# Expert capacities of 98, 88, 80 and 72 rows by rank, and four expert chunks in unused working memory

## The reference, cut to what matters

```python
def moe_swiglu(u, router_w, w1, w3, w2):
    logits = (tokens @ router_w).astype(F32)
    top_vals, top_idx = lax.top_k(logits, TOP_K)          # TOP_K = 2
    gates = jax.nn.softmax(top_vals, axis=-1)
    ...
    def run_block(args):
        tok_idx, e = args
        xb = tokens[tok_idx]
        return (jax.nn.silu(xb @ w1[e]) * (xb @ w3[e])) @ w2[e]
    ...                                                   # times the gate, added into each token's row
```

## Time and profile before

| | us |
|---|---|
| median of 3 runs (2025.71 to 2027.35) | 2026.94 |
| the profiled execution | 2017.58 |
| its span, first to last instruction | 2015.8 |
| PE busy, share of the span | 1842.4, 91% |
| PEld busy | 1510.7, 75% |
| DVE busy | 826.7, 41% |
| ACT busy | 393.1, 20% |
| DMA, moved | 480.22 MB, mean 238 GB/s |

### The profile page before, as it was taken

One profiled execution on the slowest core, in us unless ns is written; L12 is line 12 of the kernel. 1 busy time (PEld: TensorE's weight loads), 2 busy tenths in 40 slices (PEclk: granted clock), 3 DMA queues, 4 the chain that ended last, 5 costly groups with the idle time before them and its releaser, 6 DMA issues. The chain is left out here.

```text
span 2015.8 us, 43109 instructions
## 1 busy us (share of the span) xinstructions
PE 1842.4 (91%) x18202; PEld 1510.7 (75%) x18202; DVE 826.7 (41%) x2249; ACT 393.1 (20%) x1107; POOL 2.3 (0%) x6
## 2 busy tenths in 40 slices
PE   6999897999989887999999999899979998899987
PEld 4686666888868765789688998698657876688766
DVE  3756552778958812011110111110113676227661
ACT  2232333000014132000000000000012233122331
POOL 0000000000000000000000000000000000000000
PEclk7999998999989887999999999999999999899988
DMA  9622332899973123999999898999993412234100
GB/s 392 238 106 87 123 140 90 312 358 361 378 280 126 42 84 133 420 419 357 373 420 392 315 388 324 421 418 353 363 419 139 167 64 84 84 126 167 43 1 22
DMA packets 67910, 480.22 MB, mean 238 GB/s; under 512 B 7424, under 2 KB 9728, under 8 KB 9856
## 3 DMA queue, kind: packets, MB, share of 16 engines
q1 hardware_dynamic: 67712, 477.39, 60.4%
HBM read 476.31 MB, written 1.05 MB: 237 GB/s over the span
## 5 line engine op out<-in xcount | busy, mean ns | idle before, releaser
L484 PE MATMUL PS<-sb_U,sb_ring 128*128 128x256 f32 (+1 forms) x1456 | 372.6, 413 | 16.3 <-PEq L216 9.9
L484 PEld LDWEIGHTS PS<-sb_U,sb_ring 128*128 128x128 f32 x1456 | 280.7, 196 | 95.6 <-issue 59.4
L1676 PE MATMUL PS<-sb_arena,sb_ring 128*64 128x98 f32 x5632 | 246.3, 247 | 14.3 <-issue 12.2
L1676 PEld LDWEIGHTS PS<-sb_arena,sb_ring 128*64 128x64 f32 x5632 | 240.2, 136 | 21.1 <-issue 18.0
L1704 PE MATMUL PS<-sb_ring,sb_arena 128*64 128x256 f32 x1408 | 161.8, 383 | 5.1 <-issue 4.5
L755 PE MATMUL PS<-sb_U,sb_ring 128*128 128x256 f32 x704 | 155.5, 383 | 4.7 <-PEq L216 4.7
L484 PE MATMUL PS<-sb_arena 128*64 128x128 f32 (+9 forms) x884 | 150.1, 345 | 7.2 <-DVE sb_arena L717 4.4
L755 PEld LDWEIGHTS PS<-sb_U,sb_ring 128*128 128x128 f32 x704 | 134.4, 192 | 25.7 <-issue 7.4
L1704 PEld LDWEIGHTS PS<-sb_ring,sb_arena 128*64 128x64 f32 x1408 | 100.0, 137 | 54.5 <-issue 7.5
L484 PEld LDWEIGHTS PS<-sb_arena 64*128 64x128 f32 (+4 forms) x884 | 106.5, 173 | 45.2 <-issue 24.9
L340 DVE SCALAR_TENSOR_TENSOR sb_arena<-sb_ring,sb_cs,sb_arena 128x256 f32<-128x256 f32 x280 | 135.8, 485 | 10.0
(11 more groups left out here) (343 smaller groups left out, 1615.9 us busy)
## 6 DMA issues: line engine op xcount, KB each, us to landing
sb_ring<-stream SPq DMA_DIRECT2D x450, 1024.0 KB, 7.9
sb_consts<-consts SPq DMA_DIRECT2D x1, 1768.5 KB, 26.6
sb_U<-ctxT SPq DMA_DIRECT2D x1, 1024.0 KB, 6.6
sb_XT<-xT SPq DMA_DIRECT2D x1, 1024.0 KB, 8.4
out<-sb_XT SPq DMA_DIRECT2D x8, 128.0 KB, 2.0
sb_small<-small SPq DMA_DIRECT2D x1, 292.0 KB, 2.9
sb_consts<-consts SPq DMA_DIRECT2D x1, 129.0 KB, 2.8
sb_all_small<-layer_small SPq DMA_DIRECT2D x1, 110.0 KB, 26.8
```

The source lines that it names most:

```text
L484: ins = pe.transpose(o, l, r) if t.turn else pe.matmul(o, l, r, start=s, stop=e)
L1676: ins = pe.matmul(PS[c:c + 64, m % 4, h * T:h * T + n], w[:, h, kt, c:c + 64], src[:, kt, 0:n], start=(kt == 0), stop=(kt == KT - 1))
```

## The change

Three things.

**Capacities.** Ranks 0 to 3 get 98, 88, 80 and 72 rows instead of 98 each. In the order of the places that is 64, 98, 64, 88, 80, 64, 72, 64. The test before the experts counts, for each capacity, how many of the seven counts are above it, and compares with how many ranks have more.

**Four homes.** Chunks 141 to 144, the ones that pw2 used to load into freed slots, get places of their own in the arena (columns 6144, 10752, 13104 and 15968, 2048 each), with a landing semaphore each. They are issued in pw2 with no wait for a slot. Later chunks take the ring's slots as if these four were not in the stream, so pw2 now issues up to chunk 148, and 13 chunks are ready for the experts.

**Two moves.** Column 6144 is now a home, so the turned rows (`UTM`) go to `UC`, the half of `U2` that held the context and is no longer used, in the layout that a rearranged view gives. `GB`, which only `over` uses, goes to column 18016.

```diff
-RANK_CAPS = (98, 98, 98, 98, 64, 64, 64)
+RANK_CAPS = (98, 88, 80, 72, 64, 64, 64)
+STEPS = sorted(set(RANK_CAPS), reverse=True)
+LARGER = [sum(n > step for n in RANK_CAPS) for step in STEPS]
+HOMES = (6144, 10752, 13104, 15968)
+    t["caps"] = np.broadcast_to(np.array(STEPS + LARGER)[None, :], (P, 2 * len(STEPS)))
...
+    def home(self, g):
+        return g - self.home_first if self.home_first <= g < self.home_first + len(self.homes) else None
+    def turn(self, g):
+        return g if g < self.home_first else g - len(self.homes)
     def chunk(self, g):
-        return self.ring[:, (g % RING) * CH:(g % RING + 1) * CH]
+        if self.home(g) is not None:
+            return self.homes[self.home(g)]
+        slot = self.turn(g) % RING
+        return self.ring[:, slot * CH:(slot + 1) * CH]
...
+    def before(self, g):
+        if self.home(g) is not None or self.turn(g) < RING:
+            return None
+        t = self.turn(g) - RING
+        return t if t < self.home_first else t + len(self.homes)
+    def may_issue(self, g, first, end):
+        if g >= self.total:
+            return False
+        if self.home(g) is not None:
+            return first + RING >= self.home_first
+        return self.before(g) is None or self.before(g) < end
     def load(self, sp, first, n, freed):
-        last = min(first + n + RING, self.total)
-        for g in range(self.issued, last):
-            old = g - RING
-            if old >= first and old - first < n:
+        while self.may_issue(self.issued, first, first + n):
+            g, old = self.issued, self.before(self.issued)
+            if old is not None and old >= first:
                 sp.wait_ge(*freed[old - first])
-            sp.dma_start(self.chunk(g), self.dram[self.base + g]).then_inc(self.landed[g % RING], 16)
-        self.issued = max(self.issued, last)
+            sp.dma_start(self.chunk(g), self.dram[self.base + g]).then_inc(self.landing(g), 16)
+            self.issued += 1
...
+        ws = Stream(nc, ring, a["stream"], landed, [area(at, CH) for at in HOMES], home_landed, PRE_CH - OUT_CH + RING)
...
-        UTM = area(6144, 2048).rearrange("p (t n) -> p t n", t=2)
+        UTM = UC.rearrange("p k (t c) -> p t k c", t=2)
...
-                  ("dve", lambda e: e.tensor_scalar(PAIR[:, 0, :], COUNT[:, 1:8], float(HALF), None, ALU.is_gt)),
-                  ("dve!", lambda e: e.reduce_max(MOST, COUNT, AX)),
-                  ("dve", lambda e: e.reduce_sum(KEY[:, 0:1], PAIR[:, 0, :], AX)),
-                  ("dve", lambda e: e.tensor_scalar(KEY[:, 0:1], KEY[:, 0:1], NR - sum(FEW[1:]) + 0.5, None, ALU.is_gt)),
-                  ("dve", lambda e: e.scalar_tensor_tensor(out=KEY[:, 0:1], in0=COUNT[:, 0:1], scalar=float(HALF), in1=KEY[:, 0:1],
-                                                           op0=ALU.is_gt, op1=ALU.max)),
+                  ("dve", lambda e: e.tensor_tensor(PAIR[:, 0:NS, :], COUNT[:, 1:8].unsqueeze(1).broadcast_to([P, NS, NR]),
+                                                    const("caps")[:, 0:NS].unsqueeze(2).broadcast_to([P, NS, NR]), ALU.is_gt)),
+                  ("dve", lambda e: e.reduce_sum(KEY[:, 0:NS], PAIR[:, 0:NS, :], AX)),
+                  ("dve", lambda e: e.tensor_tensor(KEY[:, 0:NS], KEY[:, 0:NS], const("caps")[:, NS:2 * NS], ALU.is_gt)),
+                  ("dve", lambda e: e.reduce_max(MOST, KEY[:, 0:NS], AX)),
```

More of the change, by code:

```diff
@@ L135 @@
            ("cos64", T), ("sin64", T), ("cos32", T), ("sin32", T), ("ncum", TT * T), ("cmask", 3 * P),
-           ("fmask", T), ("bmask", T), ("cmpmask", TT * 16), ("iota", CAP), ("sel16", 16), ("one_of", 63)]
+           ("fmask", T), ("bmask", T), ("cmpmask", TT * 16), ("iota", CAP), ("sel16", 16), ("one_of", 63), ("caps", 2 * len(STEPS))]
 CONST_AT, CONST_N = offsets(CONST_W)
@@ L163, with __init__ @@
 class Stream:
-    def __init__(self, nc, ring, dram, sems):
+    def __init__(self, nc, ring, dram, sems, homes, home_sems, home_first):
         self.nc, self.ring, self.dram, self.landed = nc, ring, dram, sems
+        self.homes, self.home_landed, self.home_first = homes, home_sems, home_first
         self.used = self.issued = 0
@@ L175, in begin, with landing @@
         self.total, self.base = total, base
+    def home(self, g):
+        return g - self.home_first if self.home_first <= g < self.home_first + len(self.homes) else None
+    def turn(self, g):
+        return g if g < self.home_first else g - len(self.homes)
     def chunk(self, g):
-        return self.ring[:, (g % RING) * CH:(g % RING + 1) * CH]
-    def wait(self, eng, g):
-        eng.wait_ge(self.landed[g % RING], 16 * (g // RING + 1))
+        if self.home(g) is not None:
+            return self.homes[self.home(g)]
+        slot = self.turn(g) % RING
+        return self.ring[:, slot * CH:(slot + 1) * CH]
+    def landing(self, g):
+        return self.landed[self.turn(g) % RING] if self.home(g) is None else self.home_landed[self.home(g)]
+    def wait(self, eng, g):
+        eng.wait_ge(self.landing(g), 16 if self.home(g) is not None else 16 * (self.turn(g) // RING + 1))
+    def before(self, g):
[9 more added lines that the diff above has]
+        return self.before(g) is None or self.before(g) < end
     def load(self, sp, first, n, freed):
-        last = min(first + n + RING, self.total)
-        for g in range(self.issued, last):
-            old = g - RING
-            if old >= first and old - first < n:
+        while self.may_issue(self.issued, first, first + n):
+            g, old = self.issued, self.before(self.issued)
+            if old is not None and old >= first:
                 sp.wait_ge(*freed[old - first])
-            sp.dma_start(self.chunk(g), self.dram[self.base + g]).then_inc(self.landed[g % RING], 16)
-        self.issued = max(self.issued, last)
+            sp.dma_start(self.chunk(g), self.dram[self.base + g]).then_inc(self.landing(g), 16)
+            self.issued += 1
         self.used = first + n
     def clear(self):
-        clear_together(self.nc, self.landed)
+        clear_together(self.nc, self.landed + self.home_landed)
 class Stage:
@@ L311, in build @@
         landed = [ctx.enter_context(nc.semaphore(f"landed{i}")) for i in range(RING)]
-        ws = Stream(nc, ring, a["stream"], landed)
+        home_landed = [ctx.enter_context(nc.semaphore(f"home_landed{i}")) for i in range(len(HOMES))]
+        ws = Stream(nc, ring, a["stream"], landed, [area(at, CH) for at in HOMES], home_landed, PRE_CH - OUT_CH + RING)
         late = ctx.enter_context(nc.semaphore("late_inputs"))
@@ L1521, in build @@
         GD = area(10496, 2 * P).rearrange("p (t c) -> p t c", t=2)
-        GB = area(10752, T)
+        GB = area(18016, T)
         YG = area(13104, KT * T).rearrange("p (k t) -> p k t", k=KT)
@@ L1576, in build @@
         rk = area(15152, 560)
-        NR = NE - 1
+        NR, NS = NE - 1, len(STEPS)
         COUNT, KEY, RANK, AT = (rk[:, 8 * i_:8 * i_ + 8] for i_ in range(4))
@@ L1593, in build @@
                   ("dve!", lambda e: e.tensor_copy(COUNT, PS[:, 2, 0:8])),
-                  ("dve", lambda e: e.tensor_scalar(PAIR[:, 0, :], COUNT[:, 1:8], float(HALF), None, ALU.is_gt)),
-                  ("dve!", lambda e: e.reduce_max(MOST, COUNT, AX)),
-                  ("dve", lambda e: e.reduce_sum(KEY[:, 0:1], PAIR[:, 0, :], AX)),
-                  ("dve", lambda e: e.tensor_scalar(KEY[:, 0:1], KEY[:, 0:1], NR - sum(FEW[1:]) + 0.5, None, ALU.is_gt)),
-                  ("dve", lambda e: e.scalar_tensor_tensor(out=KEY[:, 0:1], in0=COUNT[:, 0:1], scalar=float(HALF), in1=KEY[:, 0:1],
-                                                           op0=ALU.is_gt, op1=ALU.max)),
-                  ("dve", lambda e: e.scalar_tensor_tensor(out=full_flag[:, 0:1], in0=MOST, scalar=float(CAP), in1=KEY[:, 0:1],
+                  ("dve", lambda e: e.tensor_tensor(PAIR[:, 0:NS, :], COUNT[:, 1:8].unsqueeze(1).broadcast_to([P, NS, NR]),
[3 more added lines that the diff above has]
+                  ("dve", lambda e: e.reduce_max(MOST, KEY[:, 0:NS], AX)),
+                  ("dve", lambda e: e.scalar_tensor_tensor(out=full_flag[:, 0:1], in0=COUNT[:, 0:1], scalar=float(PLACES[0][1]), in1=MOST,
                                                            op0=ALU.is_gt, op1=ALU.max))]
@@ L1614, in copy_rows @@
                 act.wait_ge(turned, j + 1)
-                nc.scalar.activation(UTM[:, t, 512 * half:512 * half + 512], PS[:, 4 + j, :], ACT.Copy)
+                nc.scalar.activation(UTM[:, t, 4 * half:4 * half + 4, :], PS[:, 4 + j, :].rearrange("p (k c) -> p k c", k=4), ACT.Copy)
         def clear_sum(pool, turned):
@@ L1639, in _ @@
             def _(sp):
-                for g in range(ws.issued, min(last_ch + RING, ws.total)):
-                    old = g - RING - first
-                    if old >= 0:
+                while ws.may_issue(ws.issued, first, last_ch):
+                    g, old = ws.issued, ws.before(ws.issued)
```

(9 more changed lines are left out.)

## The result

The changed kernel took 2010.02 us (median of 9 runs, 2004.16 to 2017.22), the kernel before 2026.89 (9 runs, 2021.53 to 2030.1): ratio 0.9931, 95% interval 0.9914 to 0.9948, or 14 us less (11 to 17). I had forecast 26, with 2001 as the time and 1984 to 2013 as the range. So it is faster, inside the range, and outside the forecast's own range of 1994 to 2008: half of the expected gain is not there.

What follows compares the result with a forecast made beforehand. TensorE and the DMA stream were taken as nearly level bounds, with instruction fetch third; savings of 3.7 + 11 + 5.5 + 0.3 + 5.5 = 26.0 us gave 2001 us, range 1984 to 2013.

Steps and rivals of the forecast that it cites:

- Homes: Place 0, first of eight expert places: four chunks loaded ahead remove 4.85 us of waits, place 1 0.6; sum 5.5 us.
- The third bound: Hidden tiles of places 3 and 6: TensorE waits for instruction blocks, about 6.15 us each behind a full DMA queue.
- The widths: Time of one matmul in places 3, 4 and 6: 38.5, 35.4 and 32.3 ns at 88, 80 and 72 columns.
- Place 6: Expert place cut to 72 rows: hidden tiles set by instruction blocks save about 0, output part 5.5 us.
- Place 3: Expert place cut to 88 rows: hidden tiles save 1 us, output tiles 2.7, sum 3.7.
- Place 4: Expert place cut to 80 rows: hidden tiles near the DMA's pace save 6 us, outputs 4.9, sum 11.
- Rival 2: Instruction fetch slower once TensorE is faster, also in place 4 and outputs: 15 us saved, 2012; chance 0.12.
- Rival 3: Place 4's queue fills, its blocks go to 6.15 us, outputs gain nothing: slower than before, 2029.5 us; chance 0.06.
- Rival 1: Gap is a price per instruction block, or fetch comes faster when asked earlier: 43 us saved, 1984; chance 0.16.

Runs made afterwards that it cites:

- experiment 2: Changed kernel with each experts-stage load bringing only half its columns, TensorE's program the same: 1945.15 us, ratio 0.9604, stage 631.5 for 703.2.
- experiment 5: Changed kernel with 16 more TensorE instructions, waits already met, in each hidden tile of the wide places: 2040.16 us, ratio 1.0082 to the kernel before.

## Why the prediction was half right

- **Homes: right.** Forecast 5.5 us, measured 5.0 in place 0. One wait of 0.56 us stayed of five, where the earlier trace rows had 4.85 us:

```profile
838.20 4.58 PE L1762 MATMUL PS<-sb_ring,sb_arena 128*64 128x128 f32 x78 [0.56 <-DMA sb_ring<-stream]
```

  SyncE issued the four home loads within 2.05 us at the stage's start, and the four of the freed slots after them, as told:

```profile
695.21 2.05 SPq L224 DMA_DIRECT2D sb_arena<-stream  x4
716.89 23.73 SPq L224 DMA_DIRECT2D sb_ring<-stream  x4
```

  The lead did no more later: place 1 is unchanged, where I had hoped for 0.6.
- **The third bound: right** in places 3 and 6, where blocks take 6.0 to 6.4 us with computing of 5.07 and 4.2 (one block takes 6.9); experiments 2 and 5 show that it is the fetch. The widths too: 5.07, 4.65 and 4.22 us for 127 matmuls less the last one's own 0.24 give 38.3, 35.0 and 31.6 ns, forecast 38.5, 35.4 and 32.3.
- **Place 6: near in the sum.** Forecast 5.5, all of it in the output part; measured 3.9, of which the hidden tiles gave 1.1 (65.5 us for 66.6) and the output part 2.8. Blocks of hidden tiles are 6.0 to 6.3 us apart with gaps of 2 us, and those gaps do a thing I had left out:

```profile
1329.51 5.80 PE L1710 MATMUL PS<-sb_arena,sb_ring 128*64 128x72 f32 x127 [2.04 <-issue]
1335.52 4.22 PE L1710 MATMUL PS<-sb_arena,sb_ring 128*64 128x72 f32 x127 [0.22 <-issue]
1341.76 4.17 PE L1710 MATMUL PS<-sb_arena,sb_ring 128*64 128x72 f32 x127 [2.02 <-issue]
```

  127 matmuls took 5.80 us for 4.22. The same columns as the earlier trace rows over the two blocks show why:

```profile
1323.00:1329.00 6.00, 4.22 (x127) 4.07 (x127) 0.91 (x4) 0.73 (x3) 0.00 (x0) 1.00 1.02 422
1329.50:1335.30 5.80, 5.79 (x127) 5.71 (x127) 0.23 (x1) 0.46 (x2) 0.00 (x0) 0.71 1.01 418
```

  The granted clock was 0.71 in the second stretch (between its two levels, 2.4 and 1.2 GHz), after a row of gaps. It costs little here, since the block behind it had arrived meanwhile and its gap is 0.22 us. In the output part blocks still wait, four times for 1.1 to 2.0 us, 5.7 together.
- **Place 3: over-sized.** Forecast 3.7, measured 0.5. The hidden tiles were to give 1 and gave -0.2 (67.6 us for 67.4). The output part was to give 2.7 and gave 0.7: three waits for blocks, of 0.39, 1.53 and 0.16 us, took 2.1 there.
- **Place 4: the step that failed.** I took 11 us: hidden tiles at the stream's 2.50 us each (6), outputs at full computing pace (4.9). It gave 0.7. The hidden tiles stayed at 2.76 us each (60.8 us in all for 60.9) and the outputs took 37.1 us for 37.6. I had seen that the block would get longer as TensorE got faster and that the two would settle at a balance; the error was to price that balance at the stream's pace. It lies at the fetch's: 5.6 us a block, while the stream's queue is only 94% busy, so the stream is not what is late. In the outputs three waits for blocks of 1.2 to 1.3 us took 3.8. One stretch behind the gap of 2.19 us lost time by the clock as well:

```profile
1179.68:1184.90 5.22, 5.22 (x102) 5.22 (x104) 0.24 (x1) 0.26 (x2) 0.00 (x0) 0.67 0.92 363
```

  I had also tied the block's length to a full queue, and that is too simple. The shares of the stream's queue and the blocks seen are: 99.3% and 6.0 to 6.9 us (place 3), 99.6% and 5.9 to 7.2 (three outstanding), 98.1% and 5.5 to 6.1 (two outstanding, place 4), 94.3% and 5.3 to 6.8 (place 4), and 96.9% and no more than 5.4 (place 4 before). The last shows that the share alone doesn't set it, nor does the time to landing, 11.9, 7.6, 5.4, 6.9 and 5.8 us in the same order. What does stays open.
- **Rivals 2 and 3.** Rival 2 (the fetch is late in place 4 and in the outputs too) has the mechanism that was measured, and I had given it 0.12. Its sum of 15 us is near the measured 14 partly by luck: it has 3.7 for place 3, 4 for place 4 and 2 for place 6, where the profile has 0.5, 0.7 and 3.9, and the stage is 10.5 us shorter. Rival 3 did not come: it wanted hidden tiles of 3.07 us and a mean block over 6.0 in place 4, and they are 2.76 and 5.6. The prediction had named the sign of either: place 4 over 95 us (97.8), first gaps there, and issue to landing over 6 us (6.9).
- **Rival 1** (the gap is a price for a block, not a floor of its length) is ruled out beside a full stream: the gap grew from 0.5 to 1.0 to 2.0 us as the block's computing shrank.
- The rule of the Trainium skill that I had weighed (Runtime: NRT & Kernel Launch, Instruction fetch mechanics: the fetch is hidden behind dispatch) agrees with the earlier trace rows, where blocks that compute for 5.4 us run with no gap. The traces of places 3, 4 and 6 after the change disagree with it, by gaps of up to 2.2 us at the blocks' ends.

## What to carry to other kernels

Before you make matmuls narrower in a fully unrolled program that streams its weights, look for gaps at a fixed count of instructions (here 256): they are a floor in time for each block, and below it fewer columns only lengthen the gap. A place that shows no gaps today may just hide the fetch behind its computing (here 5.4 us a block in place 4), and gets them when it becomes faster, with the DMA engines no busier. Loads ahead into idle memory pay at most the waits that stand before them, here 5 us for 10 us of lead.

## What the runs showed of the hardware

- A block of 256 TensorE instructions (16 KB) that TensorE waited for came 4.9 to 7.2 us after the one before, most of them 6.0 to 6.4, where the DMA engines were at least 95% busy (changed kernel; three outstanding). At 79 to 94% it was 4.7 to 6.3 us (experiment 5; three outstanding). At 70% five in a row came in 4.1 us each or less, and single ones still took 5.7 (experiment 2).
- Loads of 512 KB for 1024, cut by columns, left it at 6.1 us, and three loads outstanding for up to seven did not shorten it.
- A stream of loads into 64 partitions each moved 257 GB/s in a full queue, one into 128 partitions 420 GB/s, both in rows of 8 KB. Rows of 4 KB over 128 partitions reached 400 to 420 GB/s in the stretches where the queue was full.
- Behind gaps of 2 us the granted clock of TensorE was 0.71 over a block of 5.8 us.
- With at most two loads of 1024 KB outstanding the stream's queue was 88% busy in place 1 and 98% in place 4; with three it was 99.6% in place 1.
